# One block store, one scored piece and three norm steps moved, and a second buffer for the turned probabilities, in the mixer of a hybrid encoder layer

## The reference

```
x = x + 1/2 * SwiGLU_1(RMSNorm(x))                      # 2816 inner columns
h = RMSNorm(x);  q | k | v | u = h @ w_in               # 512 | 128 | 128 | 512 columns
attn = banded attention: chunks of 64 rows, each sees its own and the chunk before,
       8 query heads on 2 key heads, distance penalty, a learned sink per head
ssm  = S5 state space layer on u (32 groups of 16 channels, 64 complex states each),
       then z = gelu(y);  z * sigmoid(z @ w_glu + b_glu)
x = x + concat(RMSNorm(attn), RMSNorm(ssm)) @ w_out
x = x + 1/2 * SwiGLU_2(RMSNorm(x));  out = RMSNorm(x)
```

## Time and profile before

| what | value |
|---|---|
| median of three runs | 1641.88 us |
| the profiled execution's own time | 1642.36 us |
| its span, first to last instruction | 1640.7 us |
| PE busy | 1603.0 us (98%) |
| DVE busy | 1093.9 us (67%) |
| ACT busy | 712.7 us (43%) |
| POOL busy | 530.9 us (32%) |
| mean granted TensorE clock | 0.993 |

### The profile page before, as it was taken

One profiled execution on the slowest core, in us unless ns is written; L12 is line 12 of the kernel. 1 busy time (PEld: TensorE's weight loads), 2 busy tenths in 40 slices (PEclk: granted clock), 3 DMA queues, 4 the chain that ended last, 5 costly groups with the idle time before them and its releaser, 6 DMA issues.

```text
span 1640.7 us, 22012 instructions
## 1 busy us (share of the span) xinstructions
PE 1603.0 (98%) x7540; PEld 1316.5 (80%) x7540; DVE 1093.9 (67%) x1722; ACT 712.7 (43%) x1311; POOL 530.9 (32%) x953
## 2 busy tenths in 40 slices
PE   7999999999999999998999999999999999999998
PEld 5778888888888887877877778788888888888886
DVE  5866667766579887662358777765566666587765
ACT  6443443333334445521557544533433443344452
POOL 4004788877777777432030060000000000000011
PEclk8999999999999999999999999999999999999998
DMA  6345333443487545775431132233333333885443
GB/s 213 119 112 108 113 114 131 137 141 134 167 320 251 155 114 142 253 193 126 91 128 27 39 103 90 91 103 107 127 126 103 103 103 122 302 275 147 122 110 122
DMA packets 151032, 229.01 MB, mean 140 GB/s; under 512 B 18449, under 2 KB 87697, under 8 KB 147345
## 3 DMA queue, kind: packets, MB, share of 16 engines
q1 hardware_dynamic: 147856, 220.04, 41.8%
q0 software_dynamic: 3072, 7.62, 2.5%
HBM read 153.47 MB, written 74.15 MB: 139 GB/s over the span
## 4 chain that ended last, share of the span: by engine, by line
PE 57%; POOL 25%; issue 6%; DVE 5%; DMA 3%; ACT 2%; POOLq 1%; SPq 0%; DVEq 0%; ACTq 0%
PE bank L1135 18%; PE bank L1136 17%; PE bank L1137 17%; POOL pw L2958 2%; POOL EBb L3146 2%; POOL ptmp L3144 2%; POOL ptmp L3145 2%; POOL EBb L3160 2%; POOL ptmp L3159 2%; POOL ptmp L3158 2%; POOL ptmp L3104 1%; POOL ptmp L3102 1%; POOL cl_st L3108 1%; DMA par<-in_log_dt_dram 1%; DVE hblo L2296 1%
## 5 line engine op out<-in xcount | busy, mean ns | idle before, releaser
L1135 PE MATMUL bank<-hbhi,ws_lo 128*128 128x512 f32 x1056 | 413.9, 392 | 8.9 <-DVE ws_lo L2260 4.8
L1136 PE MATMUL bank<-hblo,ws_hi 128*128 128x512 f32 x1056 | 411.7, 390 | 0.0
L1137 PE MATMUL bank<-hbhi,ws_hi 128*128 128x512 f32 x1056 | 411.7, 390 | 0.0
L1135 PEld LDWEIGHTS bank<-hbhi,ws_lo 128*128 128x128 f32 x1056 | 198.8, 188 | 55.6 <-DVE ws_lo L2260 6.4
L2859 POOL TENSOR_TENSOR ssq<-ssq,sqt 128x512 f32<-128x512 f32 x25 | 34.8, 1392 | 643.5 <-ACT sqt L1661 641.3
L1135 PE MATMUL bank<-d_hi,ws_lo 128*128 128x512 f32 x616 | 240.6, 391 | 0.0
L1137 PE MATMUL bank<-d_hi,ws_hi 128*128 128x512 f32 x616 | 239.7, 389 | 0.0
L1136 PE MATMUL bank<-d_lo,ws_hi 128*128 128x512 f32 x616 | 239.7, 389 | 0.0
L1136 PEld LDWEIGHTS bank<-hblo,ws_hi 128*128 128x128 f32 x1056 | 198.8, 188 | 41.4 <-issue 0.5
L1137 PEld LDWEIGHTS bank<-hbhi,ws_hi 128*128 128x128 f32 x1056 | 198.8, 188 | 41.4
L1729 ACT ACTIVATE loc<-bank 128x512 f32<-128x512 f32 x160 | 95.6, 597 | 254.9 <-PE bank L1137 254.9
(11 more groups left out here) (298 smaller groups left out, 2620.9 us busy)
## 6 DMA issues: line engine op xcount, KB each, us to landing
b_scratch<-loc SPq DMA_DIRECT2D x42, 1024.0 KB, 7.3
d_in<-b_scratch SPq DMA_DIRECT2D x154, 256.0 KB, 3.2
raw2a<-in_ff_w_up_dram SPq DMA_DIRECT2D x44, 512.0 KB, 4.9
loc<-in_ff_w_gate_dram SPq DMA_DIRECT2D x36, 512.0 KB, 4.7
xT<-x_scratch SPq DMA_DIRECT2D x12, 1024.0 KB, 7.3
x_scratch<-xT SPq DMA_DIRECT2D x5, 2048.0 KB, 8.3
dw_lo_place<-in_ff_w_down_dram SPq DMA_DIRECT2D x8, 1024.0 KB, 7.4
x_in<-in_x_dram SPq DMA_DIRECT2D x8, 512.0 KB, 6.8
```

What stands on the lines that cost most here:

```text
L1135: nc.tensor.matmul(o, wl, rh, start=first, stop=False, skip_group_check=chain)
L1136: nc.tensor.matmul(o, wh, rl, start=False, stop=False, skip_group_check=chain)
L1137: return nc.tensor.matmul(o, wh, rh, start=False, stop=last, skip_group_check=chain)
```

## The change

- SP: `store_u(3)` is issued ahead of `load_m(1)`.
- PE: I3 moves from ahead of projection 9 to its middle, Y0 from the middle of 9 to ahead of 10. The order of the rounds, and so their banks, stay.
- PE: p0 ahead of S0 (and so each of the first pieces ahead of its scores); n0 ahead of p13, n1 behind p14.
- ACT: W13 first; C1 ahead of O0 and X2, C3 ahead of X4; n0 ahead of W17.
- DVE: W13 and p0 ahead of A0, p1 ahead of A1; B1 ahead of p2 and A2.
- `pts` becomes two buffers; the copies of tile m wait for the weighted sum m-2 in place of m-1. V7 goes to bank 0 and waits for the scores to be read (`s_biased` 16) in place of `o_taken`.
- The mixer's first norm sum goes from step 2 to step 3 of the last product, its spread from step 4 to 5.
- The spread of N_FF2's first half goes from behind piece 9 to the middle of piece 10.

```diff
--- before.py
+++ after.py
@@ -121,8 +121,8 @@
 
 
 WITH_PE = {(1, 1): steps("m1"), (4, 0): steps("E0 E1 E2 E3"), (5, 0): steps("E4 E5 E6 E7"), (6, 0): steps("K0"), (6, 1): steps("I0"),
-           (7, 0): steps("I1 K1"), (7, 1): steps("I2"), (8, 0): steps("K2"), (8, 1): steps("K3"), (9, 0): steps("I3"),
-           (9, 1): steps("Y0"), (10, 1): steps("Y1"), (11, 1): steps("Y2"), (12, 0): steps("Y3"),
+           (7, 0): steps("I1 K1"), (7, 1): steps("I2"), (8, 0): steps("K2"), (8, 1): steps("K3"), (9, 1): steps("I3"),
+           (10, 0): steps("Y0"), (10, 1): steps("Y1"), (11, 1): steps("Y2"), (12, 0): steps("Y3"),
            (13, 1): steps("v0 v1 v2 v3")}
 
 WITH_ACT = {3: steps("e0 e1 e2 e3 W3"), 4: steps("e4 e5 e6 e7 W4"), 5: steps("k0 k1 W5"), 6: steps("k2 k3"),
@@ -137,12 +137,9 @@
 GATED_DVE = [("G", 0), ("G", 1), ("G", 2), ("G", 3), ("W", 11), ("G", 4), ("G", 5), ("G", 6), ("G", 7), ("W", 12), ("R", 0), ("R", 1)]
 
 
-ATT_PE = steps("S0 p0 S1 p1 S2 p2 T0 p3 T1 V0 S3 p4 V1 S4 T2 p5 T3 V2 S5 p6 V3 S6 p7 T4 p8 T5 V4 S7 p9 V5 p10 T6 p11 T7 V6 V7"
-               " p12 p13 n0 n1 p14 r0 p15")
-ATT_ACT = steps("X0 X1 C0 W13 X2 C1 O0 X3 O1 C2 W14 X4 C3 O2 X5 O3 W15 C4 X6 C5 O4 s0 s1 X7 O5 C6 s2 s3 C7 O6 W16 O7 s4 s5 s6 s7"
-                " W17 n0 n1 h0 h1 h2 h3 W18 h4 h5 h6 h7 W19")
-ATT_DVE = steps("A0 p0 A1 B0 p1 B1 A2 W13 p2 A3 p3 B2 p4 B3 A4 W14 p5 A5 p6 B4 p7 B5 A6 W15 p8 A7 B6 p9 B7 p10 a0 W16 p11"
-                " a1 p12 W17 p13 n0 p14 h0 h1 h2 h3 p15 W18 n1 h4 h5 h6 h7 W19")
+ATT_PE = steps("p0 S0 p1 S1 p2 S2 T0 p3 T1 V0 S3 p4 V1 S4 T2 p5 T3 V2 S5 p6 V3 S6 p7 T4 p8 T5 V4 S7 p9 V5 p10 T6 p11 T7 V6 V7 p12 n0 p13 p14 n1 r0 p15")
+ATT_ACT = steps("W13 X0 X1 C0 C1 O0 X2 O1 X3 C2 W14 C3 X4 O2 X5 O3 W15 C4 X6 C5 O4 s0 s1 X7 O5 C6 s2 s3 C7 O6 W16 O7 s4 s5 s6 s7 n0 W17 n1 h0 h1 h2 h3 W18 h4 h5 h6 h7 W19")
+ATT_DVE = steps("W13 p0 A0 p1 A1 B0 B1 p2 A2 A3 p3 B2 p4 B3 A4 W14 p5 A5 p6 B4 p7 B5 A6 W15 p8 A7 B6 p9 B7 p10 a0 W16 p11 a1 p12 W17 p13 n0 p14 h0 h1 h2 h3 p15 W18 n1 h4 h5 h6 h7 W19")
 
 
 STATE_STEPS = 4 * 5 + 8
@@ -171,6 +168,7 @@
 OUT_ORDER = [(n, h) for h in range(2) for n in range(KD)]
 ATT_BANK = [0, 1, 2, 4, 5, 6]
 SSM_BANK = [6, 7, 5]
+V_BANK = [4] * 7 + [0]
 SPREAD_BANK = {(N_SSM, 0): 4, (N_SSM, 1): 5, (N_ATT, 0): 3, (N_FF2, 1): 6, (N_END, 1): 0}
 FIN_BANK = [(1, 3), (5, 7)]
 
@@ -478,7 +476,7 @@
     csn = [at(f"csn{b}", (64 + 4 * b) * KB, [P, 2, 4, NC]) for b in range(4)]
     yT = at("yT", 64 * KB, [P, 4, L])
     sco = [at(f"sco{i}", (64 + 4 * i) * KB, [P, 2, 2, 2, P]) for i in range(2)]
-    pts = at("pts", 72 * KB, [P, 2, 2, 2, P])
+    pts = [at(f"pts{i}", (72 + 4 * i) * KB, [P, 2, 2, 2, P]) for i in range(2)]
     kst = [at(f"kst{i}", (80 + 4 * i) * KB, [GH, 8, P]) for i in range(2)]
     kTp = at("kTp", 80 * KB, [P, CHUNK + L])
     biast = at("biast", 84 * KB + 512, [P, NKV, 256])
@@ -1080,8 +1078,8 @@
         load_m(0)
         store_k(1)
         load_in(7)
+        store_u(3)
         load_m(1)
-        store_u(3)
         load_u8(3)
         store_k(2)
         load_m(2)
@@ -1313,9 +1311,9 @@
         def first_half(norm):
 
             def after(what, n):
-                if (what, n) == ("step", 2):
+                if (what, n) == ("step", 3):
                     norm_sum(norm, 0)
-                elif (what, n) == ("step", 4):
+                elif (what, n) == ("step", 5):
                     norm_spread(norm, 0)
             return after
 
@@ -1470,7 +1468,9 @@
                 last.then_inc(pt_ready, 1)
 
         def weighted(m):
-            if m:
+            if m == 7:
+                pe.wait_ge(s_biased, 16)
+            elif m:
                 pe.wait_ge(o_taken, m)
             else:
                 pe.wait_ge(v_taken, 4)
@@ -1478,9 +1478,9 @@
             pe.wait_ge(pt_taken, 2 * m + 2)
             for nn in range(2):
                 for kv in range(NKV):
-                    last = nc.tensor.matmul(bank[4][kv * HD:(kv + 1) * HD, nn * 256:(nn + 1) * 256],
+                    last = nc.tensor.matmul(bank[V_BANK[m]][kv * HD:(kv + 1) * HD, nn * 256:(nn + 1) * 256],
                                             vwin[:, 2 * m + nn, kv * HD:(kv + 1) * HD],
-                                            pts[:, kv, nn, :, :].rearrange("p a q -> p (a q)"),
+                                            pts[m % 2][:, kv, nn, :, :].rearrange("p a q -> p (a q)"),
                                             start=True, stop=True)
             last.then_inc(o_ready, 1)
 
@@ -1599,9 +1599,10 @@
             if i == LAST_IN_0 + 2:
                 att_part(i, range(2))
                 norm_sum(N_FF2, 0)
-            att_part(i, (3,) if i < 3 else range(2, 4) if i == LAST_IN_0 + 2 else range(4)).then_inc(mix_out, 1)
-            if i == LAST_IN_0 + 2:
+            elif i == LAST_IN_0 + 3:
+                att_part(i, range(2))
                 norm_spread(N_FF2, 0)
+            att_part(i, (3,) if i < 3 else range(2, 4) if i in (LAST_IN_0 + 2, LAST_IN_0 + 3) else range(4)).then_inc(mix_out, 1)
 
         def out_tile(t):
             pe.wait_ge(down_taken, takes(1, N_PROD - 1) if t < 4 else 64)
@@ -1985,17 +1986,17 @@
         def p_out(m):
             for kv in range(NKV):
                 act.wait_ge(pt_ready, 2 * m + kv + 1)
-                if m:
-                    act.wait_ge(o_ready, m)
+                if m >= 2:
+                    act.wait_ge(o_ready, m - 1)
                 else:
                     act.wait_ge(h_tmp, split_before(N_ATT))
-                act.activation(pts[:, kv, :, :, :].rearrange("p n a q -> p (n a q)"), bank[2 + kv][:, :],
+                act.activation(pts[m % 2][:, kv, :, :, :].rearrange("p n a q -> p (n a q)"), bank[2 + kv][:, :],
                                ACT.Copy).then_inc(pt_taken, 1)
 
         def o_out(m):
 
             act.wait_ge(o_ready, m + 1)
-            act.activation(qT[:, 2 * m:2 * m + 2, :, :].rearrange("p n g q -> p (n g q)"), bank[4][:, :], ACT.Copy
+            act.activation(qT[:, 2 * m:2 * m + 2, :, :].rearrange("p n g q -> p (n g q)"), bank[V_BANK[m]][:, :], ACT.Copy
                            ).then_inc(o_taken, 1)
 
         def gelu(k):
```

## The result

The kernel after takes 1632.83 us (median of 5 runs, 1631.99 to 1634.41); the kernel before took 1641.99 on the same chip (1641.03 to 1644.85). The ratio is 0.9941, with a 95% interval of 0.9928 to 0.9955. The forecast was 1632.4. The profiled execution has a span of 1631.0 us for 1640.7, so 9.7 less where the sum of the parts said 9.5.

What follows compares the result with a forecast made beforehand. PE bounds the kernel, busy 1603.0 of 1640.7 us, a queue of matmuls with some 38 us of holes. Parts of 6.0 + 0.4 + 2.3 + 0.8 = 9.5 us give a forecast median of 1632.4, range 1629.3 to 1636.3.

Steps and rivals of the forecast that it cites:

- part 2: Mixer's norm: first sum a step later closes its 1.6 us hole, 1.2 given back at the second sum; net 0.4.
- part 3: Attention stretch: new lists, second buffer and V7's own bank end p15 at 930.8 for 933.1; gain 2.3 us.
- Part 1: I3's wait for u block 3: loads come 3.0 us sooner, I3 half a projection later; gain 6.0 us.
- rival C: Part 2's adds follow PE, nothing given back, more of part 3's holes close: 1.2 and up to 2 more; chance 0.15.
- A: Rival: queue full, u loads gain nothing from the reorder; part 1 is 2.3 to 4, time 1635.3; chance 0.16.
- 0.3 charged for a fuller queue: At I3: 0.3 us of waiting charged because SP's queue is fuller at 731 to 736.
- clock's share of 1.6: Behind I3's hole: granted clock 0.57 from 744 to 748, taken as 1.6 us lost that part 1 regains.
- 1.47 + 0.16 = 1.6: Mixer's first norm sum: its 1.47 idle for POOL's last add plus 0.16 per hole goes, 1.6 us.
- Rival D: ACT's table switch before n0 costs its 1.38 drain: 0.7 us less gain, 1633.1; chance within the forecast's 0.50.
- Part 4: Second block's norm spread: six matmuls ahead of it close its 0.66 wait for DVE's diagonal; gain 0.8 us.
- Rival B: Attention: softmax chain starts 1.4 late and never recovers, V3 and V5 wait longer; part 3 at 0.3, 1634.4; chance 0.13.
- E: Rival: store and u loads stick in a full queue, PE waits 13.1 us; slower by 4.9, 1646.8; chance 0.02.

Runs made afterwards that it cites:

- place undone: Kernel after with I3 ahead of projection 9 again and Y0 in its middle, SP's new order kept: 1635.34 us, ratio to before 0.9957.
- the queue experiment: Kernel after with load_m(1) issued ahead of store_u(3) on SP again, I3 keeping its new place: 1636.18 us, ratio to before 0.9957.
- the split: Kernel after with the first scores placed inside piece 0, after nine of twelve matmuls, and first maxima first on DVE: 1633.01 us, ratio to before 0.9937.
- the new lists: Kernel after with piece 0 split around the first scores and three lists reordered (scores, weighted sums, ACT's copies): 1629.14 us, ratio to before 0.9909.
- the attention part undone: Kernel after with the three old lists, one buffer of turned probabilities and V7 in bank 4: 1635.85 us, ratio to before 0.9958.

## Why the prediction was right, and where it was not

The forecast of the time was 0.4 us from the median. Part of that is luck: part 2's number came out right from wrong terms, and what part 3 fell short by (0.4) parts 1 and 2 made up (0.3 and 0.2). The ends of the stated range stand 0.1 and 0.2 above the sums that they are taken from (C's 1629.2, A's 1636.1); nothing hangs on that.

- **Part 1** was right in mechanism and nearly in size: 6.0 predicted, 6.30 measured. The data were expected at 740.8 and came at 740.54 where PE was there to meet them (place undone); PE was expected at I3 at 741.5 and was there at 741.27. The 0.3 charged for a fuller queue was not needed. The clock's share of 1.6 was real: the queue experiment has 1.5 behind a wait of only 2.5. In the second trace of the kernel before the hole is 4.88 and I2 to Y1 takes 37.34, so part 1 is worth 7.5 against that execution.
- **Part 2** is the step that failed, though its number fitted by luck (0.4 predicted, 0.6 in the two profiled executions). First, "1.47 + 0.16 = 1.6" took a wait of one execution for the kernel's. Second, "These adds hang on DVE's and ACT's lists, not on PE" is wrong for the kernel after: ACT's root waits for PE's first sum there, and the adds start 27.25 behind the old place in all nine traces, for 25.89 with the sum at step 2 and nothing late. In the kernel before they stood at 27.36 because its root was late as well (3.36), so the wait forecast at the second sum (1.2, measured 0.95) came out nearly right for a wrong reason. Last, the sum had no term for the clock, which fell behind this wait in four of nine traces, at 1.6 each. Part 2 looks like a loss of about 1.0 and not a gain of 0.4.
- **Part 3** was 2.3 predicted, 1.93 measured. Right: V7's wait goes whole, T2 0.5, V3 and V5 stay (0.70 and 0.71 for 0.95 and 0.8), p15 without a new wait. Wrong: T0 was to gain 0.5 and gained 0.02. The low part cost 0.50 and not 0.2: on the old clock time piece 0 began at 855.17 (848.28 + 6.89) and not at 855.3, and DVE's split ended at 857.72 (849.68 + 1.15 + 6.89) and not at 857.55. S0 stood 1.8 later than on the old order, and the first maxima with it (1.4 predicted), so the chain reached T0 0.5 later than the walk had it. T3's expected 0.3 is 0.15 or less.
- The rule of the Trainium skill ("ScalarE: Activation LUTs", What ACT_TABLE_LOAD costs) that each switch also drains for 1.38 us is not what this trace shows: the load at 914.51 takes 1.28 and the root starts at 915.80, and r0 has no wait. Rival D falls. Timeline of ACT:

```profile
912.83 1.66 ACT L1662 ACTIVATE sqt_a<-qT 128x512 f32<-128x512 f32 x3
914.51 1.28 ACT L1671 ACT_TABLE_LOAD   x1
915.80 0.26 ACT L1671 ACTIVATE std<-bank,eps_t 128x4 f32<-128x4 f32 x1
```

- **Part 4**: 0.8 predicted, 0.90 and 0.89 measured.
- Rival B (the chain never recovers) fell with V3 and V5 no worse than before; rival C was right that part 2's adds follow PE, but wrong that nothing is given back by it, and wrong on part 3's holes; E did not happen: with the place undone the data came 2.0 us behind the last u issue (734.83 + 3.70 to 740.54).

## What to carry to other kernels

A wait that an independent engine with slack ends (POOL's long chain here) differs from one execution to the next. Before a sum is moved for it, look at a second trace, follow what hangs on that sum, and price the place that it is moved to. Where one operand of a step is late by less than a step, split the step there rather than swap two steps: here either order left a hole at that place, and the split none. In written lists, try the order before adding a bank or buffer: the new lists took away 3.8 us with the split, 0.9 of them by the split, and the added bank 0.8.

## What was not expected of the hardware

How PE's clock answers a wait is not set by the wait's length alone. Granted clocks behind a wait, by trace:

- after 0.92 to 0.96 us at the second norm sum it fell in four of nine traces (0.57 to 0.68 in 680 to 684) and stayed at 1.00 in five;
- after 0.44 there, after 0.88 at the spread and after 1.47 at the first norm sum it stayed, in one trace each;
- after 1.58 to 1.65 at the first scores it fell in two of four;
- after 1.73 or 1.74 at V7 it did not fall within the next 5 us in any of three;
- after 1.87 at I3 it stayed, after 2.50, 4.61 and 4.88 it was down.

The two traces that fell at the scores had fallen at the second norm sum as well, the other two had no wait there. One fall, in 924 to 928 with the attention part undone, has only 0.17 us of idle and the two short norm sums just ahead of it; the two traces of the kernel before have the same list there and stay at 1.00. A fall cost about 1.6 us, with PE otherwise busy, at the lower of its two levels; behind the 4.88 it cost 2.5. I can't say from these runs what decides it. For a forecast it means that a small hole on PE costs its length, and in some executions 1.6 us more.
